# Turning 64-column tiles into both halves of PSUM instead of first doubling them in SBUF, in a two-block transformer kernel

## The chip, the core and the metric

The kernel runs on one core of one Trainium2 chip. Its time is the device time of one execution in microseconds, given as the median of three runs. The engines named below are PE (TensorE, the matrix engine), ACT (ScalarE), DVE (VectorE), POOL (GpSimd) and SP (SyncE, which here issues the weight transfers). SBUF is the on-chip memory with 128 partitions; PSUM holds the results of the matrix engine in eight banks, each 512 f32 numbers wide in every partition.

## The reference, cut to what matters

Sequence length 512, model width 1024, head size 64, everything in f32. The first block has differential attention, an attention with compressed, selected and windowed keys ("NSA") and an MLP. The second block has forget-gated attention ("fox") and sliding-window attention with sinks ("swa"), whose four key heads are each shared by four query heads. Two pieces matter here.

```
# 1. compression of the NSA keys (kc) and values (vc): 4 groups of 64 columns, windows of 32 tokens, stride 16
k_cmp = compress(kc.reshape(B, S, G, HEAD_DIM), cmp_pos_k[l], cmp_k_w1[l], cmp_k_w2[l])
v_cmp = compress(vc.reshape(B, S, G, HEAD_DIM), cmp_pos_v[l], cmp_v_w1[l], cmp_v_w2[l])
#    for each group and each of 31 windows: the 32 x 64 numbers of the window, plus a position term,
#    times a [2048, 256] matrix, GELU, times a [256, 64] matrix

# 2. scores of the swa block: 16 query heads against 4 key heads
logits = jnp.einsum('bnqhgd,bnkhd->bnhgqk', qb, k_band) * scale
```

## The kernel before, in words

Every large product is split into groups of 512 output columns; a group has two units of weights, each 512 rows deep. ACT and DVE split the weights of a unit into a high and a low part (`spl`), and PE multiplies three times (high-high, high-low, low-high). A unit is 48 such matmuls on PE. The results of a group lie in four PSUM banks, and ACT copies ("evicts") them into `QKV`, where tokens lie along the partitions. There are two slots for unit weights and two sets of four banks, so each engine works in an order that is written out by hand, one list per engine. Semaphores tie the lists together. `run(...)` walks the groups of a stage. Its arguments `at` and `between` put other work ahead of a group or behind a unit.

The stage `nsa_in` has the groups pd0, pd1, kc, nq0, nq1, ks, kw and ng, numbered 0 to 7. The group kc brings 256 columns of keys and 256 of values to be compressed. The compression needs, for each of the 32 token positions of a window, the 64 columns of a token along the partitions. Two token positions are packed together: one in partitions 0 to 63, the next in partitions 64 to 127, so that its first layer is 16 matmuls deep instead of 32 for each half of the hidden columns. The kernel before gets the packing in this way:

- ACT evicts kc twice (`token_twice`, line 760), so that every 64-column group lies twice side by side, in 128 columns of `QKV` (1536 to 2560).
- PE turns these 128-column tiles (`tokens_across`, line 2113): 16 transposes for the keys after unit 0 of group nq0, and 16 for the values after unit 0 of group ks. Both halves of the partitions then hold the same 64 columns.
- DVE copies windows out of partitions 0 to 63 (`inputs`, line 1696) and ACT those out of partitions 64 to 127 (`inputs`, line 1057), 16 copies each of 64 x 124 numbers. A constant, the position term, is added. The partitions of ACT's half are read one token further (`window`).
- PE may not begin group nq1 (number 4) before the first set of copies is done, and not group kw (number 6) before the second (`gathered`), since these groups write the banks that the copies read. The first layer (`first_layer`, line 2124) is 32 matmuls, once for the keys and once for the values.

In the swa block the same doubling is done for keys. Each of the eight units of that attention works on two query heads, one in partitions 0 to 63 and one in 64 to 127, against one key head that must lie in both halves. POOL copies the four key heads twice into columns 2560 to 3072 (`keys_twice`, line 1962), between the normalization of the keys and that of the first query group. PE turns a 128-column tile (`turn`, line 2453) for queries (argument `i` = 0) in every unit and for keys (`i` = 1) in every second unit. The first three such turns stand ahead of the loop; the others stand inside it, two steps ahead of the unit that needs them. PE waits for POOL's copies through the semaphore `k_twice`.

Of the kernel before, what the change touches and what calls it, by code (L numbers as in the profile page):

```python
# [22 lines left out]
ALU = mybir.AluOpType  # L23
ACT = mybir.ActivationFunctionType
AX = mybir.AxisListType

P = 128
S = 512
NT = S // P
D = 1024  # L30
KT = D // P
HD = 64
# [223 lines left out]
def program(nc, I, out):  # L256
    RUNS = plan()
    LAST = {a: [g for r in RUNS.values() for g in r if g["by"] == a][-1]["freed"] for a in ("act", "dve")}
    with ExitStack() as ctx:
# [12 lines left out]
        def sem(name):  # L272
            return ctx.enter_context(nc.semaphore(name))
# [118 lines left out]

        ck_zero, k_twice, c_xk2 = sem("ck_zero"), sem("k_twice"), sem("c_xk2")
        x_parked, x_back = sem("x_parked"), sem("x_back")
# [12 lines left out]
        def c_bank(k):  # L407

            return 4 * ((RUNS["nsa_in"][0]["group"] + k) % 2)
# [84 lines left out]
        def row_bank(name):  # L494

            return 4 * (1 - RUNS["merge"][0]["group"] % 2) + 3 if name == "merge" else 4 * (SIDE[name]["group"] % 2) + 3

        def token_twice(t):

            return QKV[:, t, 1536:2560].rearrange("p (g r d) -> p g r d", r=2, d=HD)  # L500

        def window(i, k, r):

            b, rows, o = c_bank(6 if i else 4), slice(HD * r, HD * r + HD), 2 * k + r
            return (XK[rows, k], PS[rows, b:b + 4, o:o + 1 + CMP_STRIDE * (N_CMP - 1):CMP_STRIDE],
                    POS[rows, i, k:k + 1])

# [167 lines left out]
        def _(act):  # L675
# [48 lines left out]
            def evict(g):  # L724
# [29 lines left out]
                if then[0] in ("norm", "plain"):  # L754
                    k = g["late"]
                    act.wait_ge(*row_count(k))
                    for t in range(NT):
                        if g["name"] == "kc":
                            for r in range(2):
                                last = act.activation(token_twice(t)[:, :, r],  # L760
                                                      PS[:, b0 + t].rearrange("p (g d) -> p g d", d=HD),
                                                      ACT.Copy, scale=RST[:, k, t:t + 1])
                            continue
                        last = act.activation(QKV[:, t, then[1]:then[1] + W], PS[:, b0 + t], ACT.Copy,  # L764
                                              scale=RST[:, k, t:t + 1])
                    last.then_inc(freed["act"], 1)
# [282 lines left out]

            def inputs(i):  # L1050

                act.wait_ge(c_tr, i + 1)
                if i:
                    act.wait_ge(c_hid, 1)
                for k in range(16):
                    dst, src, add = window(i, k, 1)
                    act.activation(dst, src, ACT.Identity, bias=add).then_inc(c_xk2, 1)

            def hidden(i):
# [49 lines left out]
            def lambdas():  # L1109
# [7 lines left out]
            run(RUNS["nsa_in"], primed=True, at={3: lambda: narrow_hi(0, 48), 7: compressed},  # L1117
                between={3: lambda: inputs(0), 4: lambda: hidden(0), 5: lambda: inputs(1), 6: keys_out_values_in})
            compressed_branch()
# [20 lines left out]
        def _(dve):  # L1140
# [548 lines left out]
            def inputs(i):  # L1689

                dve.wait_ge(c_tr, i + 1)
                if i:
                    dve.wait_ge(c_hid, 1)
                for k in range(16):
                    dst, src, add = window(i, k, 0)
                    dve.tensor_scalar(dst, src, add, None, ALU.add).then_inc(c_xk, 1)  # L1696

# [99 lines left out]
        def _(pool):  # L1797
# [157 lines left out]

            def keys_twice():

                pool.wait_ge(n_done, RUNS["swa_in"][0]["normed"] + 1)
                keys = QKV[:, :, 1024:1280].rearrange("p t (h d) -> p t h d", d=HD)
                both = QKV[:, :, 2560:3072].rearrange("p t (h r d) -> p t h r d", r=2, d=HD)  # L1960
                for r in range(2):
                    last = pool.tensor_copy(both[:, :, :, r], keys)
                last.then_inc(k_twice, 1)

            def clear_narrow(last):
# [22 lines left out]
            attend_beside(FOX)  # L1988
            run(RUNS["swa_in"][:1])
            keys_twice()  # L1990
            run(RUNS["swa_in"][1:])
            attend_beside(SWA)
# [3 lines left out]
        def _(pe):  # L1996
# [109 lines left out]
            def tokens_across(i):  # L2106


                pe.wait_ge(freed["act"], RUNS["nsa_in"][4 if i else 2]["freed"])
                for g in range(GROUPS):  # L2110
                    b, c = c_bank(6 if i else 4) + g, 1536 + 512 * i + P * g
                    for t in range(NT):
                        last = pe.transpose(PS[:, b, P * t:P * t + P], QKV[:, t, c:c + P], IDF[:])
                last.then_inc(c_tr, 1)

            def first_layer(i):
                b = c_bank(7 if i else 5) + 2 * i
                pe.wait_ge(freed["act"], RUNS["nsa_in"][5 if i else 3]["freed"])
                pe.wait_ge(w1_full, 16 * (4 if i else 3))
                for m in range(2):  # L2120
                    for k in range(16):
                        pe.wait_ge(c_xk, 16 * i + k + 1)
                        pe.wait_ge(c_xk2, 16 * i + k + 1)
                        last = pe.matmul(PS[:, b, 124 * m:124 * m + 124], W1[:, k, P * m:P * m + P],
                                         XK[:, k].rearrange("p g n -> p (g n)"), start=(k == 0), stop=(k == 15),
                                         skip_group_check=True)
                last.then_inc(c_hid, 1)
# [202 lines left out]
            def attend_beside(a):  # L2330
# [117 lines left out]
                def turn(m, i):  # L2448
                    for t in range(NT):
                        bank, col = (first_bank(a, m, i), P * t) if m < 2 else (turn_bank(a, X_BANK), P * t) if a.is_diff \  # L2450
                            else (turn_bank(a, PT_BANK + t // 2), 256 + P * (t % 2))
                        c = 2560 + P * a.keys_of(m) if i and a.is_swa else 1024 * i + P * m
                        last = pe.transpose(PS[:, bank, col:col + P], QKV[:, t, c:c + P], IDF[:])
                    last.then_inc(s["tk" if i else "tq"], 1)
# [22 lines left out]
                pe.wait_ge(n_done, last_in[{"diff": 3, "fox": 4, "swa": 1}[a.name]]["normed"] + 1)  # L2477
                if a.is_swa:
                    pe.wait_ge(k_twice, 1)
                for m, i in a.first_turns()[:3]:  # L2480
# [32 lines left out]

            def gathered(i):
                pe.wait_ge(c_xk, 16 * i + 16)
                pe.wait_ge(c_xk2, 16 * i + 16)

            pe.wait_ge(loads, 16 * N_LOADS)
            run(RUNS["nsa_in"], at={4: lambda: gathered(0), 5: lambda: pe.wait_ge(c_gelu, 1), 6: lambda: gathered(1)},
                between={(0, 0): lambda: back(KT - 1), (3, 0): lambda: tokens_across(0), (4, 0): lambda: first_layer(0),  # L2520
# [63 lines left out]
```

## Time and profile before

| | |
|---|---|
| median of 3 runs | 1770.33 us (1769.92 to 1773.02) |
| the profiled execution's own time | 1769.92 us |
| its span in the profile | 1768.1 us |
| PE busy | 1678.7 us, 95% of the span, 9314 matmul records |
| DVE, ACT, POOL busy | 933.9, 726.6 and 383.9 us |
| mean granted PE clock | 0.966 of full speed |

Times in the profile are microseconds from the start of the span. A row of a timeline gives the start, the time from the start of the first to the end of the last instruction of a merged group, the engine, the line in the code, what is written and read, the shape, how many records (x16), and in brackets how long the engine had been idle and what ended that. On PE consecutive matmuls overlap at their ends, so the pace of a group is best read from its start to the start of the next group. In the names of a matmul's operands the moving one stands first, the stationary one second; "128\*64" is a stationary operand of 128 rows and 64 columns. A plain f32 matmul leaves two records, a transpose or one of the split matmuls leaves one. The granted clock (PEclk) is 1.00 at the full 2.4 GHz and 0.50 at 1.2 GHz.

### The profile page before, as it was taken

How to read it: one execution, taken by the hardware profiler on the slowest of the kernel's cores; microseconds unless marked ns; L12 is line 12 of the kernel's file. 1: busy time of each engine (PE TensorE's matmuls, PEld its weight loads, DVE VectorE, ACT ScalarE, POOL GpSimd, SP SyncE). 2: the span in 40 equal slices, each digit the busy share in tenths (PEclk: the TensorE clock that was granted, in tenths of full speed). 3: DMA queues.
4: the chain of work that ended last, by engine and by line, in shares of the span. 5: the costliest groups of instructions: out<-in, count | busy, mean ns of one | idle time of the engine just before them, and what ended most of it. 6: DMA issues, size and time to landing. Idle time of an engine off the chain costs nothing.

```text
span 1768.1 us, 24731 instructions
## 1 busy us (share of the span) xinstructions
PE 1678.7 (95%) x9314; PEld 1318.8 (75%) x9314; DVE 933.9 (53%) x1675; ACT 726.6 (41%) x1643; POOL 383.9 (22%) x517
## 2 busy tenths in 40 slices
PE   7999998998879998999999999999999989997989
PEld 6887667887755555888888888888887767885757
DVE  3785674356346666344443244234836774457772
ACT  4324553143336665224332133133325553434550
POOL 5451332023125663011000000000113330022330
PEclk9999998999959999999999999999999998998979
DMA  7222002423012222322322333223230004230111
GB/s 187 96 78 90 25 25 83 143 93 122 1 42 58 62 59 67 126 102 83 95 97 99 101 101 104 96 77 138 96 97 25 26 25 143 96 95 2 49 49 48
DMA packets 107205, 141.38 MB, mean 80 GB/s; under 512 B 30348, under 2 KB 55204, under 8 KB 106848
## 3 DMA queue, kind: packets, MB, share of 16 engines
q1 hardware_dynamic: 106032, 139.10, 24.6%
q0 software_dynamic: 992, 0.86, 0.5%
q8 instruction: 69, 1.13, 0.3%
q14 instruction: 32, 0.26, 0.0%
q10 hardware_dynamic: 80, 0.02, 0.0%
HBM read 125.24 MB, written 4.24 MB: 73 GB/s over the span
## 4 chain that ended last, share of the span: by engine, by line
PE 67%; DVE 11%; issue 10%; ACT 9%; POOL 3%; DMA 0%; ACTq 0%; SPq 0%; POOLq 0%; DVEq 0%
PE ps L2010 50%; PE ps L2462 3%; PE ps L2245 2%; PE ps L2266 2%; ACT pbd L948 2%; DVE spl L1163 2%; DVE nm L1491 2%; PE ps L2281 1%; PE ps L2419 1%; ACT pb L892 1%; DVE qkt L1509 1%; PE ps L2443 1%; ACT qkt L969 1%; PE ps L2351 1%; ACT pts L956 1%
## 5 line engine op out<-in xcount | busy, mean ns | idle before, releaser
L2010 PE MATMUL ps<-spl,ht 128*128 128x512 f32 x2496 | 578.4, 393 | 10.3 <-DVE xk L1696 5.9
L2010 PEld LDWEIGHTS ps<-spl,ht 128*128 128x128 f32 x2496 | 472.7, 190 | 110.1 <-DVE xk L1696 6.3
L1186 DVE TENSOR_TENSOR spl<-raw,spl 128x1024 fp32r<-128x1024 f32 x168 | 222.1, 1364 | 396.3 <-ACT spl L721 396.3
L721 ACT ACTIVATE spl<-raw 128x1024 fp32r<-128x1024 f32 x168 | 168.5, 1052 | 463.5 <-PE ps L2010 437.2
L2010 PE MATMUL ps<-ht,spl 128*128 128x512 f32 x960 | 220.4, 391 | 2.0 <-DVE spl L1186 2.0
L2010 PEld LDWEIGHTS ps<-ht,spl 128*128 128x128 f32 x960 | 181.2, 189 | 40.5 <-issue 2.9
L2010 PE MATMUL ps<-spl,uu 128*128 128x512 f32 x768 | 174.7, 389 | 0.0
L2010 PEld LDWEIGHTS ps<-spl,uu 128*128 128x128 f32 x768 | 144.1, 188 | 29.8
L2462 PE MATMUL ps<-ht,spl 128*128 128x512 f32 x576 | 155.2, 408 | 2.7 <-DVE mx L1546 2.6
L1872 POOL TENSOR_TENSOR sq<-qkv 128x2048 f32<-128x2048 f32 (+1 forms) x15 | 51.5, 3434 | 326.0 <-ACT qkv L764 311.4
L2462 PEld LDWEIGHTS ps<-ht,spl 128*128 128x128 f32 x576 | 102.7, 190 | 23.8 <-DVE mx L1546 4.8
L1968 POOL MEMSET nws<- 128x2048 f32 x2 | 3.6, 1812 | 426.6 <-PE ps L2010 385.1
L1903 POOL TENSOR_TENSOR pb<-pb,rg 128x512 f32<-128x512 f32 (+3 forms) x128 | 89.4, 720 | 5.0
L1491 DVE TENSOR_REDUCE nm<-ps 128x1 f32<-128x512 f32 (+2 forms) x192 | 81.2, 450 | 8.9 <-PE ps L2368 6.5
L892 ACT ACTIVATE pb<-ps,nm 128x512 f32<-128x512 f32 (+3 forms) x128 | 66.4, 528 | 29.2 <-DVE nm L1411 29.2
L2351 PE MATMUL ps<-qkt 64*128 64x256 f32 (+3 forms) x576 | 68.0, 343 | 9.8 <-DVE qkt L1509 9.6
L1411 DVE TENSOR_REDUCE nm<-ps 128x1 f32<-128x512 f32 (+3 forms) x128 | 56.9, 486 | 35.7 <-PE ps L2250 35.6
L2351 PEld LDWEIGHTS ps<-qkt 64*128 64x128 f32 x576 | 43.4, 192 | 43.2 <-issue 32.1
L1949 POOL TENSOR_TENSOR pbf<-pbf,rr 128x512 f32<-128x512 f32 (+3 forms) x64 | 48.8, 783 | 121.1 <-DVE rr L1498 121.1
L1881 POOL TENSOR_TENSOR sq<-qkv,st 128x1024 f32<-128x1024 f32 (+3 forms) x22 | 49.1, 2253 | 63.6 <-DVE qkv L1236 63.6
L2443 PE MATMUL ps<-pts,qkv 128*64 128x128 f32 x544 | 47.8, 303 | 14.3 <-ACT pts L956 11.7
L1163 DVE SCALAR_TENSOR_TENSOR spl<-raw,spl 128x256 fp32r<-128x256 f32 x80 | 45.4, 576 | 23.9 <-ACT spl L698 23.1
(311 smaller groups left out, 2223.5 us busy)
## 6 DMA issues: line engine op xcount, KB each, us to landing
raw<-w_in SPq DMA_DIRECT2D x30, 1024.0 KB, 5.1
raw<-w_mlp_up SPq DMA_DIRECT2D x16, 1024.0 KB, 5.3
raw<-w_mlp_down SPq DMA_DIRECT2D x16, 1024.0 KB, 5.0
raw<-w_in_a SPq DMA_DIRECT2D x16, 1024.0 KB, 5.4
raw<-w_in_b SPq DMA_DIRECT2D x8, 1024.0 KB, 5.5
raw<-w_proj_diff SPq DMA_DIRECT2D x4, 1024.0 KB, 6.8
stq<-qkv SPq DMA_DIRECT2D x16, 256.0 KB, 2.7
stq<-qkv SPq DMA_DIRECT2D x32, 128.0 KB, 2.5
```

The costliest lines, as they stand in the source:

```text
L721: act.activation(SPL[:, n % 2, HI, 2 * k:2 * k + 2], RAW[:, n % 2, 2 * k:2 * k + 2], ACT.Copy).then_inc(hi_done, 4)
L892: last = act.activation(p, PS[:, 2 * (idx % 2) + h, 0:w], ACT.Exp, bias=NM[:, m.slot, h, t:t + 1], accum_out=LS[:, m.slot, h, t:t + 1])
L1163: last = dve.scalar_tensor_tensor(wide(SPL[:, n % 2, LO])[:, k], wide(RAW[:, n % 2])[:, k], gain, wide(SPL[:, n % 2, HI])[:, k].bitcast(F3 ...
L1186: dve.tensor_tensor(SPL[:, n % 2, LO, 2 * k:2 * k + 2], RAW[:, n % 2, 2 * k:2 * k + 2], SPL[:, n % 2, HI, 2 * k:2 * k + 2].bitcast(F32), A ...
L1411: dve.tensor_reduce(top, bank[:, 0:w], AX.X, ALU.max, negate=True).then_inc(s["mx"], 1)
L1491: dve.tensor_reduce(NM[:, m % 2, h, t:t + 1], bank[:, 0:w + a.sink], AX.X, ALU.max, negate=True)\
L1872: pool.tensor_tensor(SQ[:, :, 0:w], QKV[:, :, col:col + w], QKV[:, :, col:col + w], ALU.mult)\
L1903: last = pool.tensor_tensor(p, p, RG[:, m.slot, h, t:t + 1].to_broadcast([P, w]), ALU.mult)
L2010: last = pe.matmul(PS[:, b0 + b], left[:, x], right[:, y], start=(kt == 0 and i == 0), stop=(kt == UK * g["units"] - 1 and i == 2))
L2351: pe.matmul(PS[:, score_bank(a, n, h), 0:w], QKT[r, m % 2, 0, x, P * t:P * t + P], QKT[r, a.keys_of(m) % 2, 1, y, P * a.first_key(t):P * t ...
L2443: last = pe.matmul(PS[HD * h:HD * h + HD, turn_bank(a, PV_BANK), P * t:P * t + P], QKV[:, j, v:v + HD], PTS[h][:, n % 2, o:o + P], start=( ...
L2462: last = pe.matmul(PS[:, side_bank(a, k)], wide(SPL[:, n % 2, x])[:, kt, cols], HT[:, y, kt], start=(kt == 0 and j == 0), stop=(kt == KT - ...
```

## The change

The doubling in SBUF goes away. Where both halves of the partitions must hold the same 64 columns, PE now does two operations on the 64-column tile. A transpose writes partitions 0 to 63, and an ordinary f32 matmul against the identity writes partitions 64 to 127.

```
 def tokens_across(i):
-    pe.wait_ge(freed["act"], RUNS["nsa_in"][4 if i else 2]["freed"])
+    kc = RUNS["nsa_in"][2]
+    pe.wait_ge(freed["act"], kc["freed"])
+    if i:
+        pe.wait_ge(freed["act"], RUNS["nsa_in"][4]["freed"])
     for g in range(GROUPS):
-        b, c = c_bank(6 if i else 4) + g, 1536 + 512 * i + P * g
+        b = c_bank(6 if i else 4) + g
+        src = QKV[:, :, 1024 + 256 * i + HD * g:1024 + 256 * i + HD * g + HD]
         for t in range(NT):
-            last = pe.transpose(PS[:, b, P * t:P * t + P], QKV[:, t, c:c + P], IDF[:])
+            n = P - (t == NT - 1)
+            pe.transpose(PS[0:HD, b, P * t + 1:P * t + 1 + n], src[0:n, t], IDF[0:n, 0:n])
+            last = pe.matmul(PS[HD:P, b, P * t:P * t + P], src[:, t], IDF[:], start=True, stop=True,
+                             skip_group_check=True)
```

The transposed half is written one column further, so both token positions of a window stand in the same columns, and one copy over all 128 partitions takes both. DVE does all the copies, and ACT's `inputs` is gone:

```
 dve.wait_ge(c_tr, i + 1)
 if i:
     dve.wait_ge(c_hid, 1)
+b = c_bank(6 if i else 4)
 for k in range(16):
-    dst, src, add = window(i, k, 0)
-    dve.tensor_scalar(dst, src, add, None, ALU.add).then_inc(c_xk, 1)
+    src = PS[:, b:b + 4, 2 * k + 1:2 * k + 2 + CMP_STRIDE * (N_CMP - 1):CMP_STRIDE]
+    dve.tensor_scalar(XK[:, k], src, POS[:, i, k:k + 1], None, ALU.add).then_inc(c_xk, 1)
```

ACT's double eviction of kc becomes the ordinary one. `keys_twice` on POOL is gone with its semaphore, and the turn of the swa keys is changed like the other:

```
-                        if g["name"] == "kc":
-                            for r in range(2):
-                                last = act.activation(token_twice(t)[:, :, r],
-                                                      PS[:, b0 + t].rearrange("p (g d) -> p g d", d=HD),
-                                                      ACT.Copy, scale=RST[:, k, t:t + 1])
-                            continue
...
-            run(RUNS["swa_in"][:1])
-            keys_twice()
-            run(RUNS["swa_in"][1:])
+            run(RUNS["swa_in"])
...
-                        c = 2560 + P * a.keys_of(m) if i and a.is_swa else 1024 * i + P * m
-                        last = pe.transpose(PS[:, bank, col:col + P], QKV[:, t, c:c + P], IDF[:])
+                        if i == 0 or not a.is_swa:
+                            c = 1024 * i + P * m
+                            last = pe.transpose(PS[:, bank, col:col + P], QKV[:, t, c:c + P], IDF[:])
+                            continue
+                        k = QKV[:, t, 1024 + HD * a.keys_of(m):1024 + HD * a.keys_of(m) + HD]
+                        pe.transpose(PS[0:HD, bank, col:col + P], k, IDF[:])
+                        last = pe.matmul(PS[HD:P, bank, col:col + P], k, IDF[:], start=True, stop=True,
+                                         skip_group_check=True)
```

How this stands on PE at two places. First, in `nsa_in`, from the end of unit 0 of nq0 to the first layer for the keys (`xk` is the gathered windows, `w_88` the first layer's weights, `spl` and `ht` the operands of the large products). Before:

```order
L2010 MATMUL ps<-spl,ht 128x512 x144
L2113 MATMUL ps<-idf,qkv 128x128 x16
L2010 MATMUL ps<-spl,ht 128x512 x96
L2124 MATMUL ps<-xk,w_88 128x124 x32
L2010 MATMUL ps<-spl,ht 128x512 x96
```

And now, where the two lines 2083 and 2084 alternate 16 times, of which the first and the last stand here:

```order
L1975 MATMUL ps<-spl,ht 128x512 x144
L2083 MATMUL ps<-idf,qkv 64x128
L2084 MATMUL ps<-idf,qkv 64x128
...
L2083 MATMUL ps<-idf,qkv 64x127
L2084 MATMUL ps<-idf,qkv 64x128
L1975 MATMUL ps<-spl,ht 128x512 x96
L2095 MATMUL ps<-xk,w_88 128x124 x32
L1975 MATMUL ps<-spl,ht 128x512 x96
```

Each set of 16 transposes has become 16 transposes of half the width and 16 matmuls, and the place in the row is the same. Second, in the loop of the swa block, at one of the three key turns that stand inside it (`pts` is the transposed probabilities, `pbs` the probabilities, `ht` and `spl` the gate's product that runs beside). Before:

```order
L2443 MATMUL ps<-pts_69,qkv 64x128
L2453 MATMUL ps<-idf,qkv 128x128 x4
L2419 MATMUL ps<-idf,pbs_83 128x128 x2
L2462 MATMUL ps<-ht,spl 128x512 x6
L2351 MATMUL ps<-qkt 128x256 x6
```

And now:

```order
L2414 MATMUL ps<-pts_69,qkv 64x128
L2428 MATMUL ps<-idf,qkv 64x128
L2429 MATMUL ps<-idf,qkv 64x128
...
L2428 MATMUL ps<-idf,qkv 64x128
L2429 MATMUL ps<-idf,qkv 64x128
L2390 MATMUL ps<-idf,pbs_83 128x128 x2
L2439 MATMUL ps<-ht,spl 128x512 x6
L2322 MATMUL ps<-qkt 128x256 x6
```

Four transposes have become four pairs of a transpose and a matmul. Nothing else on PE changes its place.

## Rows read from the trace of the kernel before

**Rows 1.** The page: the span, and busy time of each engine.

```profile
span 1768.1 us, 24731 instructions
PE 1678.7 (95%) x9314; PEld 1318.8 (75%) x9314; DVE 933.9 (53%) x1675; ACT 726.6 (41%) x1643; POOL 383.9 (22%) x517
```

**Rows 2.** Timeline of PE, 355 to 440 us: the compression inside `nsa_in`.

```profile
362.46 1.91 PE L2113 MATMUL ps<-idf,qkv 128*128 128x128 f32 x16
364.13 22.05 PE L2010 MATMUL ps<-spl,ht 128*128 128x512 f32 x96
386.02 7.30 PE L2124 MATMUL ps<-xk,w 128*128 128x124 f32 x64
393.08 22.02 PE L2010 MATMUL ps<-spl,ht 128*128 128x512 f32 x96
...
416.60 11.14 PE L2010 MATMUL ps<-spl,ht 128*128 128x512 f32 x48
433.65 6.62 PE L2010 MATMUL ps<-spl,ht 128*128 128x512 f32 x22 [5.90 <-DVE xk L1696]
```

**Rows 3.** Chain that ended last, 400 to 440 us: start, duration, what.

```profile
418.12 6.70 POOL sq L1881 x2
...
429.45 4.15 DVE xk L1696 x16
```

**Rows 4.** Timeline of ACT, 340 to 445 us.

```profile
354.27 4.71 ACT L760 ACTIVATE qkv<-ps,rst 128x512 f32<-128x512 f32 x8
363.02 2.01 ACT L721 ACTIVATE spl<-raw 128x1024 fp32r<-128x1024 f32 x2 [4.04 <-PE ps L2010]
```

**Rows 5.** Groups of DVE by shape: xcount | busy us, mean ns | idle.

```profile
L1621 DVE TENSOR_TENSOR ys<-y,ys 128x512 fp32r<-128x512 f32 x8 | 4.9, 681 | 0.0
...
L1669 DVE TENSOR_TENSOR crem<-cum,c 16x512 f32<-16x512 f32 x1 | 0.7, 678 | 0.0
```

**Rows 6.** Timeline of PE, 1388 to 1398 us, in the fox block.

```profile
1390.87 1.09 PE L2443 MATMUL ps<-pts,qkv 128*64 128x128 f32 x16
1391.89 0.88 PE L2419 MATMUL ps<-idf,pbf 128*128 128x128 f32 x6
```

**Rows 7.** Timeline of PE, 1268 to 1272 us: turning 16 columns.

```profile
1269.72 0.60 PE L2536 MATMUL ps<-idf,fl 128*16 128x128 f32 x4
1270.08 2.30 PE L2010 MATMUL ps<-spl,ht 128*128 128x512 f32 x9
```

**Rows 8.** Stretches: PE, PEld, DVE, ACT, POOL busy, PEclk, DMA share, GB/s.

```profile
434.00:436.00 2.00, 2.00 (x6) 1.52 (x6) 2.00 (x2) 0.00 (x0) 0.28 (x1) 0.50 0.00 0
436.00:438.00 2.00, 2.00 (x9) 1.64 (x8) 2.00 (x6) 0.00 (x0) 0.00 (x0) 0.88 0.29 23
```

**Rows 9.** The same view, 697 to 701 us.

```profile
697.00:699.00 2.00, 0.06 (x2) 0.00 (x0) 1.90 (x3) 2.00 (x3) 0.00 (x0) 1.00 0.02 2
699.00:701.00 2.00, 1.93 (x5) 1.59 (x6) 2.00 (x2) 2.00 (x5) 0.00 (x0) 0.58 0.36 39
```

**Rows 10.** Timeline of POOL, 1530 to 1620 us.

```profile
1553.76 2.03 POOL L1962 COPY qkv<-qkv 128x1024 f32<-128x1024 f32 x2 [5.40 <-DVE qkv L1260]
1563.82 3.60 POOL L1872 TENSOR_TENSOR sq<-qkv 128x2048 f32<-128x2048 f32 x1 [8.02 <-ACT qkv L764]
```

**Rows 11.** Timeline of PE, 1530 to 1620 us: the start of the swa attention.

```profile
1581.29 1.47 PE L2453 MATMUL ps<-idf,qkv 128*128 128x128 f32 x12
...
1602.58 1.01 PE L2351 MATMUL ps<-qkt 64*128 64x256 f32 x6 [8.90 <-DVE qkt L1509]
```

**Rows 12.** Timeline of PE, 1640 to 1656 us: a key turn in the loop.

```profile
1648.48 0.65 PE L2453 MATMUL ps<-idf,qkv 128*128 128x128 f32 x4
1648.97 0.38 PE L2419 MATMUL ps<-idf,pbs 128*128 128x128 f32 x2
...
1652.51 0.63 PE L2419 MATMUL ps<-idf,pbs 128*128 128x128 f32 x4 [0.31 <-POOL pbs L1949]
```

**Rows 13.** Waits of PE, 1600 to 1770 us: total, times, longest.

```profile
PE ps L2419 <- POOL pbs L1949: 0.6, 2, 0.3
```

More of the change, by code:

```diff
@@ L391, in need @@
             return BESIDE[k], n + (0 if a.is_diff else IN_DIFF[k]) + (IN_FOX[k] if a.is_swa else 0)
-        ck_zero, k_twice, c_xk2 = sem("ck_zero"), sem("k_twice"), sem("c_xk2")
+        ck_zero = sem("ck_zero")
         x_parked, x_back = sem("x_parked"), sem("x_back")
@@ L496, in row_bank @@
             return 4 * (1 - RUNS["merge"][0]["group"] % 2) + 3 if name == "merge" else 4 * (SIDE[name]["group"] % 2) + 3
[L498 to L506, printed above, removed]
         def reach(eng, s, value):
@@ L1048, in split_y @@
                     act.activation(YS[:, HI, k], Y[:, k], ACT.Copy).then_inc(y_hi, 1)
[L1050 to L1057, printed above, removed]
             def hidden(i):
@@ L1117, in _ @@
             run(RUNS["nsa_in"], primed=True, at={3: lambda: narrow_hi(0, 48), 7: compressed},
-                between={3: lambda: inputs(0), 4: lambda: hidden(0), 5: lambda: inputs(1), 6: keys_out_values_in})
+                between={4: lambda: hidden(0), 6: keys_out_values_in})
             compressed_branch()
@@ L1954, in attend_beside @@
                     root(KT - 1)
[L1956 to L1963, printed above, removed]
             def clear_narrow(last):
@@ L2122, in first_layer @@
                         pe.wait_ge(c_xk, 16 * i + k + 1)
-                        pe.wait_ge(c_xk2, 16 * i + k + 1)
                         last = pe.matmul(PS[:, b, 124 * m:124 * m + 124], W1[:, k, P * m:P * m + P],
@@ L2477, in attend_beside @@
                 pe.wait_ge(n_done, last_in[{"diff": 3, "fox": 4, "swa": 1}[a.name]]["normed"] + 1)
-                if a.is_swa:
-                    pe.wait_ge(k_twice, 1)
                 for m, i in a.first_turns()[:3]:
@@ L2512, in keys_out_values_in @@
                 narrow(RUNS["nsa_in"][-1], 0)
-            def gathered(i):
-                pe.wait_ge(c_xk, 16 * i + 16)
-                pe.wait_ge(c_xk2, 16 * i + 16)
             pe.wait_ge(loads, 16 * N_LOADS)
-            run(RUNS["nsa_in"], at={4: lambda: gathered(0), 5: lambda: pe.wait_ge(c_gelu, 1), 6: lambda: gathered(1)},
+            run(RUNS["nsa_in"], at={4: lambda: pe.wait_ge(c_xk, 16), 5: lambda: pe.wait_ge(c_gelu, 1),
+                                    6: lambda: pe.wait_ge(c_xk, 32)},
                 between={(0, 0): lambda: back(KT - 1), (3, 0): lambda: tokens_across(0), (4, 0): lambda: first_layer(0),
```

## The prediction

> **What bounds the kernel now.** The page comes first: PE is busy 1678.7 of 1768.1 us [rows 1], so an operation put on PE costs its own time unless PE waits soon after it, and one taken off another engine is worth only what PE waited for it. The timeline of PE through the compression comes next. PE runs without a gap from the first transposes at 362.46 to the end of ks at 427.7, then stands idle 5.90 us until DVE's window copies are done [rows 2]. The chain of waits shows what made these copies late. It passes through POOL's products for the rotation of nq1 (418.12) to the copies at 429.45 [rows 3]: DVE first finishes the normalization of nq1, which PE completed before it turned the values, and then turns to the copies. So the end of the wait hangs on PE's end of nq1, not on the turn of the values that follows it. ACT's half of the copies is never named. The third place is the swa block: PE waits 8.90 us before its first scores and almost nothing inside the loop [rows 11 to 13].
>
> **What a turn costs, before and now.** The 16 transposes take 364.13 - 362.46 = 1.67 us, 0.104 each [rows 2]. Now each tile has a transpose and an f32 matmul of 128 columns, which leaves two records. The nearest price of such a record is the first layer's: 64 records in 393.08 - 386.02 = 7.06 us, 0.110 each, so a matmul takes 0.22 [rows 2]. No row shows a transpose of 64 columns. One of only 16 columns is no cheaper than a whole one: four in 1270.08 - 1269.72 = 0.36 us, 0.09 each [rows 7]. I take 0.104, half the width being no saving.
>
> The open question is whether the two overlap. They write different halves of the partitions. Matmuls that do so already stand in the trace: 16 records of L2443, which alternate between the halves, take 1391.89 - 1390.87 = 1.02 us, 0.064 each [rows 6]. That is little over half of the 0.110 of a record that fills all 128 columns. Two at a time they would take 16 x 0.055 = 0.88, and 0.14 us is what such a group pays once. So two matmuls in different halves run at the same time. If a transpose in one half overlaps with the matmul in the other in the same way, a pair lasts as long as the half with more to do: 0.22. If not, 0.104 + 0.22 = 0.324. With nearly nothing to tell them apart I choose the row of the same shape, which overlaps: 0.22 a pair, and 0.1, most of that 0.14, once for a group.
>
> Here the Trainium skill speaks against the change. Its page "TensorEngine Tiling (Array Packing)", section "Key Properties", says that changing the tiling mode drains the engine, and section "Gotcha 2: Feature Incompatibilities" that column tiling excludes transpose mode for f32 input. By the second, the transposes would have to leave the tiled mode, and by the first each pair would pay for draining twice. The 16-column f32 transposes, with their usual cost, speak against it [rows 7], but none of them stands next to a tiled matmul. So I keep it as a rival below.
>
> **The change part by part.**
> - *Turn of the keys to be compressed.* 16 x 0.22 + 0.1 = 3.6 us instead of 1.67: +1.95 us. PE has no gap before it reaches the end of nq1, which starts the chain to the 433.65 wait. So the whole 1.95 is exposed. It moves everything behind it. Bounds: 48 records at 0.064 are 3.1, +1.4; without overlap 16 x 0.324 + 0.1 = 5.3, +3.6.
> - *Turn of the values.* The same +1.95, but after the end of nq1 and before the 5.90 us idle, whose end does not depend on it: 0. Some 4.0 us of idle are left (2.3 without overlap). Were that cover gone, it would cost as much as the first.
> - *The clock.* PE's granted clock is 0.50 from 434 to 436 and on average 0.88 from 436 to 438, so the work from 433.65 to about 436.5 ran at 1.2 GHz, where the same work takes twice its time: some 1.4 us lost [rows 8]. A shorter idle time could save it. But elsewhere the clock fell after a stall of only about 2 us: idle from 697 to 699 at 1.00, then 0.58 [rows 9]. I take 0; bounds -1.4 and +0.3.
> - *Window copies.* DVE keeps its 16 per set, now over 128 partitions instead of 64. DVE's time does not follow the partitions: 512 columns take 678 ns on 16 partitions and 681 ns on 128 [rows 5]. So 4.15 us stays, 0. At the other end, if twice the partitions took twice as long, the second set would add 4.15 us, all exposed. ACT's 32 copies go, and nobody waited for them: 0. The first layer now waits for one semaphore per step instead of two. Its 0.110 per record is 0.006 above a transpose's 0.104, so at most 128 x 0.006 = 0.8 us is to be had. I take 0.
> - *Eviction of kc.* ACT does 4 instead of 8, saving half of 4.71 us; ACT then sat idle 4.04 us until PE freed a weight slot [rows 4]. Nobody waited: 0.
> - *POOL's doubling of the swa keys.* 2.03 us at 1553.76, after which POOL idled 8.02 us until an eviction [rows 10]. 0, and PE's removed wait had long been satisfied.
> - *First key turn of swa.* One third of the 12 transposes at 1581.29: +0.5, hidden behind the 8.90 us that end with DVE [rows 11]. 0; it costs 0.5 (0.9 without overlap) if uncovered.
> - *Three key turns in the loop.* Each takes 1648.97 - 1648.48 = 0.49 now [rows 12], and 4 x 0.22 + 0.1 = 0.98 then: +0.49, three times 1.47. PE has next to no gap in the loop, so this is exposed, except that one step after two of the three PE waits 0.3 us for POOL's scaled probabilities (1652.51 is one), 0.6 in all, which start from scores PE has done before the turn [rows 12, 13]. 1.47 - 0.6 = +0.9. Bounds: 3 x (12 x 0.064 - 0.49) - 0.6 = +0.2 and, without overlap, 3 x (1.296 + 0.1 - 0.49) - 0.6 = +2.1.
>
> **Sum.** 1.95 + 0.9 = +2.85 us on a profiled execution of 1769.92 (span 1768.1 and 1.8 around it). That execution was 0.4 below the median of 1770.33. I forecast the median: 1773.2 us.
>
> **Rivals.**
> - *No overlap* (slower). A transpose and a matmul in different halves run one after the other. Place: the key turn and the three turns in the loop. Price: 3.6 + 2.1 = +5.7 us, 1776.0. For it: no row shows the two kinds side by side. Against: the same shape overlaps among matmuls [rows 6]. With p us a pair the sum is 16p - 1.57 + 12p - 1.77 = 28p - 3.34, so it decides from p = 0.25 on, where the sum passes 3.5 us.
> - *Draining* (slower). Each pair pays what a group of matmuls in halves pays once, 0.14 us [rows 6], on top of no overlap: 0.464 a pair, +5.85 for the key turn, 3 x (1.856 + 0.1 - 0.49) - 0.6 = +3.8 in the loop: +9.65, 1780.0. The value turn stays just covered: 5.85 against 5.9. This is what the page of the Trainium skill named above would lead to.
> - *Cheap records and a saved clock* (not slower). Every record at 0.064: +1.4 + 0.2 = +1.6. If then the shorter idle keeps the clock, -1.4: 1770.5. Against: two records in a row into the same half have no row at that pace, and the stall of 2 us speaks against the clock [rows 9].
> - *Copies that grow with the partitions* (slower): 2.85 + 4.15 = +7.0, 1777.3. Rows 5 leave it little.
>
> **Chances and range.** Overlap 0.50, no overlap 0.27, draining 0.11, cheap 0.09, growing copies 0.03. A measurement tells 0.2% from no change, 3.5 us. The forecast at +2.85 lies inside it by only 0.7, and phases of the clock and the spread of the runs move it by about 1, so 0.13 of its 0.50 go to slower. With no overlap 0.25, draining 0.11 and growing copies 0.02, slower gets 0.51. Faster by 3.5 us needs more than any edit here frees on PE: 0.04. The same: 0.45. The range runs from 1771.0 to 1778.0; it holds the forecast, the case without overlap and most of the growing copies, and leaves out draining and the best of cheap. The forecast's own range is 1771.8 to 1774.5.
>
> **What would show it.** In the trace after, the key turn lasts 3.6 us from its start to the next large matmul (5.3: no overlap; 7 and more: draining). The idle time before kw shrinks from 5.9 to about 4.0 and still ends with DVE's copies, whose 16 last 4.15 us. The clock dips there as before. The swa stage has a wait of about 8.4 us before its first scores, key turns of 1.0 us in the loop, and the two 0.3 us waits for POOL are gone. I am wrong if PE's new wait is for ACT or POOL at a place that had none, or if the turn of the values shows up in the start of kw.

## The result, and the profile after

The changed kernel takes 1781.78 us (median of 5, 1779.92 to 1784.85). The kernel before, run beside it, takes 1772.39 (median of 5). By the medians that is +9.4 us. The ratio over all executions, 30 of the changed kernel, is 1.0058, interval 1.0047 to 1.0069: 8.3 to 12.2 us slower. The forecast was 1773.2, the range 1771.0 to 1778.0, so the time lies outside. About 2 us of the distance come from the kernel before, which the forecast took at 1770.33. The profiled execution took 1782.82, its span is on the first line of the page:

```profile
span 1781.0 us, 24819 instructions
PE 1702.4 (96%) x9410; PEld 1329.2 (75%) x9410; DVE 933.5 (52%) x1675; ACT 717.1 (40%) x1607; POOL 382.4 (21%) x515
```

Against [rows 1], PE has 96 more records and 23.7 us more busy time. That is 0.25 per record; the forecast's turns added 1.95 us for 32 records, 0.06 each, and without overlap 0.11. ACT and POOL have less to do, as the change says. The timeline of PE through the compression, which answers to [rows 2], shows where the time is:

```profile
365.27 0.27 PE L2083 MATMUL ps<-idf,qkv 128*64 128x128 f32 x1
365.47 0.43 PE L2084 MATMUL ps<-idf,qkv 128*64 128x128 f32 x2
365.84 0.30 PE L2083 MATMUL ps<-idf,qkv 128*64 128x128 f32 x1
366.07 0.43 PE L2084 MATMUL ps<-idf,qkv 128*64 128x128 f32 x2
...
374.36 0.43 PE L2084 MATMUL ps<-idf,qkv 128*64 128x128 f32 x2
374.72 22.07 PE L1975 MATMUL ps<-spl,ht 128*128 128x512 f32 x96
...
425.55 0.27 PE L2083 MATMUL ps<-idf,qkv 128*64 128x128 f32 x1
...
435.00 22.07 PE L1975 MATMUL ps<-spl,ht 128*128 128x512 f32 x96
456.91 0.54 PE L2103 MATMUL ps<-w2s,hid 128*124 128x64 f32 x4
```

L2083 is the transpose, L2084 the matmul beside it (two records). Read the starts, since the durations hold the pipeline's depth. From a transpose to its matmul it is 0.20 to 0.23 us, from the matmul to the next transpose 0.36 or 0.37: 0.59 a pair. The 16 pairs of the keys last 374.72 - 365.27 = 9.45 us, where 1.67 stood and 3.6 was forecast. The 16 of the values last the same. The 5.90 us idle before kw is gone: the 96 large matmuls of ks and kw follow each other without a gap.

The weight loads of PE (PEld, LDWEIGHTS) show where the time between the two kinds lies:

```profile
365.05 0.11 PEld L2083 LDWEIGHTS ps<-idf,qkv 128*64 128x64 f32 x1
365.47 0.19 PEld L2084 LDWEIGHTS ps<-idf,qkv 128*64 128x64 f32 x2 [0.32 <-issue]
365.83 0.11 PEld L2083 LDWEIGHTS ps<-idf,qkv 128*64 128x64 f32 x1 [0.17 <-issue]
```

The loads sit idle 0.32 and 0.17 us ahead of the last two of these rows, waiting for nothing that the profile names. The load of each kind starts only at the time (365.47, 365.83) at which PE's own record begins, with nothing loaded ahead while the other kind streams. The very first transpose is different: its weights are loaded at 365.05, 0.22 us before it starts at 365.27, while the large matmuls ahead of it still run. The chain of waits, which went through POOL and DVE before [rows 3], now stays on PE:

```profile
425.71 0.11 PE ps L2083
425.82 0.36 PE ps L2084 x2
```

DVE's 16 copies for the values, now over 128 partitions, and ACT's eviction and next work, which answer to [rows 3 to 5]:

```profile
439.93 4.15 DVE L1672 TENSOR_SCALAR xk<-ps,pos 128x124 f32<-128x124 f32 x16
```

```profile
357.09 2.40 ACT L748 ACTIVATE qkv<-ps,rst 128x512 f32<-128x512 f32 x4
365.55 2.00 ACT L711 ACTIVATE spl<-raw 128x1024 fp32r<-128x1024 f32 x2 [6.06 <-PE ps L1975]
```

The copies take 4.15 us as before and end at 444.08, some 2 us before PE comes to kw near 446.0. ACT does its eviction in half the time and waits 6.06 instead of 4.04. And since PE did not stall, its clock (the 1.00 behind POOL's busy time) stays full at the place of [rows 8]:

```profile
446.00:448.00 2.00, 2.00 (x10) 1.66 (x9) 0.60 (x1) 1.69 (x2) 0.00 (x0) 1.00 0.03 8
```

In the swa attention, in answer to [rows 11, 12]:

```profile
1612.37 1.01 PE L2322 MATMUL ps<-qkt 64*128 64x256 f32 x6 [6.95 <-DVE qkt L1484]
...
1659.61 0.28 PE L2428 MATMUL ps<-idf,qkv 128*64 128x128 f32 x1
...
1661.95 0.44 PE L2390 MATMUL ps<-idf,pbs 128*128 128x128 f32 x2
...
1732.10 10.12 PE L1975 MATMUL ps<-spl,ht 128*128 128x512 f32 x35
```

A key turn takes 2.34 us instead of 0.49, and the wait before the first scores is 6.95 instead of 8.90: the first turn's extra 1.95 is hidden there, as forecast. The waits of PE no longer name POOL ([rows 13]).

Two more starts on PE in the kernel before, the second layer and the end of swa's loop, serve to lay the traces side by side:

```profile
446.00 0.54 PE L2132 MATMUL ps<-w2s,hid 128*124 128x64 f32 x4
...
1719.18 11.04 PE L2010 MATMUL ps<-spl,ht 128*128 128x512 f32 x39
```

The traces drift apart like this, each by the start of the same instruction: at the keys' first transpose by 2.8 us (stretches of half clock in the first 170 us that lie differently in these two executions, ahead of any change), after them by 10.6, at the second layer (446.00 and 456.91) by 10.9, at the first scores of swa by 9.8, at the end of its loop (1719.18 and 1732.10) by 12.9. So the keys' turn costs +7.8, the values' turn +0.3 net, the swa loop +3.1. That is 11.2 us, inside the interval. Between the second layer and swa's first scores the changed kernel gains 1.1 us in these two executions. It does so in work that the change doesn't touch, for the most part where the granted clock changes (near 508 and 1470 us); it is not counted.

### The profile page after: what moved, and what is told of

Same layout as the page of the kernel before. It is cut to its first block, busy times and chain, and to the rows that moved or that the text cites. A ratio compares the mean times of both kernels' runs of the same rounds, so it can differ in the third digit from the quotient of the medians.

```text
span 1781.0 us, 24819 instructions
## 1 busy us (share of the span) xinstructions
PE 1702.4 (96%) x9410; PEld 1329.2 (75%) x9410; DVE 933.5 (52%) x1675; ACT 717.1 (40%) x1607; POOL 382.4 (21%) x515
## 4 chain that ended last, share of the span: by engine, by line
PE 77%; DVE 9%; ACT 8%; issue 4%; POOL 1%; DMA 0%; ACTq 0%; SPq 0%; POOLq 0%; DVEq 0%
PE ps L1975 55%; PE ps L2439 3%; PE ps L1967 2%; PE ps L2216 2%; PE ps L2237 2%; ACT pbd L932 2%; DVE nm L1466 1%; PE ps L2252 1%; DVE spl L1138 1%; PE ps L2322 1%; PE ps L2390 1%; PE ps L2414 1%; ACT pb L876 1%; ACT pbf L932 1%; PE ps L2095 1%
## 5 line engine op out<-in xcount | busy, mean ns | idle before, releaser
L2414 PE MATMUL ps<-pts,qkv 128*64 128x128 f32 x544 | 48.0, 304 | 13.6 <-ACT pts L940 10.6
```

The costliest lines, as they stand in the source:

```text
L2414: last = pe.matmul(PS[HD * h:HD * h + HD, turn_bank(a, PV_BANK), P * t:P * t + P], QKV[:, j, v:v + HD], PTS[h][:, n % 2, o:o + P], start=( ...
```

## The experiments

The traces say what a pair costs, not why. Theory A (as the expectations call it) is that each step between a transpose and an ordinary matmul costs by itself. Its rivals: the transpose with 64 columns is slow, going back and forth between the halves of the partitions is slow, or any change of kind is slow, at full width too. All times are medians, but for two kernels that ran once; the kernel before took 1772.2 to 1772.4 on the same chips.

**Grouping the kinds.** Per four tiles first all transposes, then all matmuls, in the compression and in swa.

```
                     for t in range(NT):
                         pe.transpose(PS[0:HD, ...], src[0:n, t], IDF[0:n, 0:n])
+                    for t in range(NT):
                         last = pe.matmul(PS[HD:P, ...], src[:, t], IDF[:], ...)
```

> The changed kernel with the same operations in another order: for each four tiles first the four transposes into partitions 0 to 63, then the four matmuls into 64 to 127, in both turns of the compression and in all swa key turns. In the trace of the changed kernel a pair took 0.59 us, 0.23 from transpose to matmul and 0.36 from matmul to transpose, against 0.104 + 0.22 without anything between. Theory A, the going from a transpose to a matmul and back costs some 0.13 us each time: two such steps per four tiles instead of eight, so four tiles take 4 x 0.104 + 8 x 0.11 + 2 x 0.13 = 1.56 us instead of 2.37, the key turn 6.2 instead of 9.45 us, and the kernel is about 5 us faster than the changed one (about 1777). Theory B, each 64-column operation is slow in itself: four tiles stay at 2.4 us, the time at 1782. Theory C, going from one half of the partitions to the other costs: the same as A.

1774.58 us, ratio to before 1.0016 (1.0006 to 1.0026). The same operations in another order save 7 of the 9 us; 5 were expected. Its timeline of PE:

```profile
362.31 0.60 PE L2083 MATMUL ps<-idf,qkv 128*64 128x128 f32 x4
362.84 1.09 PE L2085 MATMUL ps<-idf,qkv 128*64 128x128 f32 x8
363.86 0.63 PE L2083 MATMUL ps<-idf,qkv 128*64 128x128 f32 x4
...
368.59 9.79 PE L1975 MATMUL ps<-spl,ht 128*128 128x512 f32 x42
...
438.03 9.36 PE L1975 MATMUL ps<-spl,ht 128*128 128x512 f32 x40 [1.19 <-DVE xk L1672]
```

Four tiles take 363.86 - 362.31 = 1.55 to 1.58 us with two steps, where eight steps took 4 x 0.59 = 2.36. So a step costs (2.36 - 1.58) / 6 = 0.13 us. What is left is 1.58 - 0.26 = 1.32 for four tiles, 0.33 each: a 64-column transpose of 0.11 and a matmul of 0.22, one after the other. The transpose itself isn't slow. The last row is the start of kw: 1.19 us of idle are left of 5.90, since the values' turn now fills more of it.

**Two matmuls.** Both halves by ordinary matmuls, at all sites; no transposes.

```
-                        pe.transpose(PS[0:HD, ...], src[0:n, t], IDF[0:n, 0:n])
+                        pe.matmul(PS[0:HD, ...], src[0:n, t], IDF[0:n, 0:n], start=True, stop=True, ...)
```

> The changed kernel with both halves written by ordinary f32 matmuls against the identity, in the same order tile by tile. There is no transpose left among the 64-column operations, but the halves still alternate. Theory A (a step between transpose and matmul costs): no step is left, both halves overlap as in L2414's groups at 0.064 us a record, so 16 tiles take 64 x 0.064 = 4.1 us instead of 9.45, four tiles 1.0 to 1.1 instead of 2.4, and the kernel comes to about 1773, 9 us faster than the changed one and within 1 or 2 us of the kernel before. Theory B (the 64-column operations are slow in themselves, 0.36 us a matmul): 32 x 0.36 = 11.6 us, slower than the changed kernel by 2 us or more. Theory C (going to the other half costs 0.13): 32 x (0.22 + 0.13) = 11 us, slower too.

1773.21 us, ratio 1.0008 (0.9998 to 1.0017): +1.0 us over the 1772.22 of the kernel before. That it lies on the forecast's 1773.2 is chance, since the forecast added 2.85 to 1770.33. The price of a pair is what this kernel puts to the test, and its timeline of PE shows it:

```profile
364.38 0.32 PE L2083 MATMUL ps<-idf,qkv 128*64 128x128 f32 x1
364.39 0.32 PE L2085 MATMUL ps<-idf,qkv 128*64 128x128 f32 x1
...
368.02 2.35 PE L1975 MATMUL ps<-spl,ht 128*128 128x512 f32 x9
```

The two halves start 0.01 us apart and a pair takes 0.22: 3.64 us for all 16, where 3.6 was forecast for the change. Going back and forth between halves costs nothing. So overlap is real for two matmuls, and missing for a transpose and a matmul. Theory B and Theory C are both out.

**Steps at full width.** The kernel before, with every second of the compression's whole-width transposes as a plain matmul.

```
-                        last = pe.transpose(PS[:, b, ...], QKV[:, t, c:c + P], IDF[:])
+                        if t % 2: last = pe.matmul(PS[:, b, ...], QKV[:, t, c:c + P], IDF[:], ...)
+                        else: last = pe.transpose(PS[:, b, ...], QKV[:, t, c:c + P], IDF[:])
```

> The kernel before, in whose two turns of the compression every second one of the 16 full-width (128-column) transposes is an ordinary f32 matmul against the identity, into all 128 partitions; output unchanged. Read from the start of the 16 operations to the next large matmul. If the step between a transpose and a matmul costs 0.13 us whatever the width: 8 x 0.104 + 8 x 0.22 + 16 x 0.13 = 4.7 us. If it costs only where the operations fill half of the columns: 2.6 us. The time: +3.0 or +1 us over the kernel before.

1770.40 us (one execution, within the spread of the kernel before, so that the time says nothing here). Timeline of PE, and then of its weight loads:

```profile
362.83 0.27 PE L2117 MATMUL ps<-idf,qkv 128*128 128x128 f32 x1
362.94 0.39 PE L2114 MATMUL ps<-idf,qkv 128*128 128x128 f32 x2
363.17 0.27 PE L2117 MATMUL ps<-idf,qkv 128*128 128x128 f32 x1
...
365.27 0.39 PE L2114 MATMUL ps<-idf,qkv 128*128 128x128 f32 x2
365.41 0.94 PE L2010 MATMUL ps<-spl,ht 128*128 128x512 f32 x3
```

```profile
363.06 0.14 PEld L2117 LDWEIGHTS ps<-idf,qkv 128*128 128x128 f32 x1
```

A pair takes 0.33 or 0.34 us, 0.11 + 0.22, with 16 steps among them, and all of them take 365.41 - 362.83 = 2.58 us, as the second case had it (2.6 against 4.7). At full width a step is free. The next kind's weights are loaded before the other's stream ends (363.06, for a record that starts at 363.17). That is what the changed kernel's loads don't do.

**Steps inside one half.** In the lower half transpose and matmul in turn (T M T M), then four matmuls for the upper half; compression only.

```
+                        if t % 2: pe.matmul(PS[0:HD, ...], src[0:n, t], IDF[0:n, 0:n], ...)
+                        else: pe.transpose(PS[0:HD, ...], src[0:n, t], IDF[0:n, 0:n])
+                    for t in range(NT):
                         last = pe.matmul(PS[HD:P, ...], src[:, t], IDF[:], ...)
```

> The changed kernel, in whose two turns of the compression the lower half of each four tiles is written by transpose, matmul, transpose, matmul, and then the upper half by four matmuls. All steps between transpose and matmul but one per four tiles are now inside one half of the partitions. Theory A (the step between the kinds costs 0.13 us among 64-column operations, whichever half they write): four steps per four tiles, 2 x 0.104 + 2 x 0.22 + 3 x 0.22 + 4 x 0.13 = 1.8 to 2.0 us for four tiles. Theory E (it costs only where the step also changes the half): one such step, 1.4 to 1.6 us. The time is not the question: about 2 us below the changed kernel.

1779.36 us (one execution). Timeline of PE:

```profile
365.23 0.27 PE L2087 MATMUL ps<-idf,qkv 128*64 128x128 f32 x1
365.43 0.43 PE L2084 MATMUL ps<-idf,qkv 128*64 128x128 f32 x2
365.79 0.30 PE L2087 MATMUL ps<-idf,qkv 128*64 128x128 f32 x1
366.02 0.32 PE L2084 MATMUL ps<-idf,qkv 127*64 127x127 f32 x1
366.03 0.32 PE L2089 MATMUL ps<-idf,qkv 128*64 128x128 f32 x1
...
367.04 0.30 PE L2087 MATMUL ps<-idf,qkv 128*64 128x128 f32 x1
```

L2087 and L2084 write the same half, and yet the steps are the 0.20 to 0.23 and 0.36 of the changed kernel. At 366.02 a lower and an upper matmul start together. Four tiles take 367.04 - 365.23 = 1.81 us, in the 1.8 to 2.0 of Theory A and not the 1.4 to 1.6 of Theory E. What costs is the change of kind among 64-column operations, whichever half it writes.

The ends of the turns in the changed kernel narrow this down. Ahead of the first transpose stand large matmuls, which are ordinary ones at full width. That change of kind is free: the weights are loaded ahead (365.05), and the transpose starts 0.23 us after the last large matmul, which is the pace of the large ones (22 us for 96). Behind the last 64-column matmul stands a large matmul again, which is no change of kind. Yet it comes only 0.36 us later (374.36 to 374.72), as late as a transpose would, where the same step at full width takes 365.41 - 365.27 = 0.14. The 0.14 us that a group of L2443 pays once [rows 6] is of the same kind, and there the neighbours behind are transposes of 128 columns. So the price hangs on going into and out of 64-column ordinary matmuls. A 64-column transpose stands on the side of the full-width operations: from them to it nothing is paid.

**The three places alone.** On the kernel before, the transpose and matmul pair only in swa's key turns (without the doubling), only in the values' turn, only in the keys' turn. The edit is the change's own line for one place, here the keys':

```
+                        if i == 0:
+                            pe.transpose(PS[0:HD, b, ...], QKV[:, t, c:c + HD], IDF[:])
+                            last = pe.matmul(PS[HD:P, b, ...], QKV[:, t, c:c + HD], IDF[:], ...)
```

> The kernel before with the change made in the swa block alone (key turns of transpose and matmul, POOL's doubling gone), the compression as before. By the trace of the changed kernel the three key turns in the loop take 2.37 instead of 0.49 us each, 5.6 in all, less 0.6 and 0.2 of waits that disappear and less what the first, covered turn does not add: I expect +3 to +5 us over the kernel before (1775 to 1777), and so +5 to +6 of the whole +9.4 for the compression. Rival: POOL's 2 us are worth something after all, and the swa block is neutral.

> The kernel before, with only the turn of the values changed into 16 pairs of a transpose and a matmul; doubling, copies and everything else as before. The turn then takes 9.45 instead of 1.67 us, +7.8, against 5.90 us of idle time before the group kw. By the trace of the changed kernel 1.9 us stick out, and the clock loss of 1.4 us or more goes with the wait: +0 to +1 us over the kernel before. Rival: it is exposed in full, +7.8.

> The kernel before, with only the turn of the keys to be compressed changed into 16 pairs of a transpose and a matmul. Theory: all of it is exposed, 9.45 - 1.67 = +7.8 us over the kernel before (1780), the wait of 5.9 us before the group kw stays as it is, and only moves. Together with the swa turns (+3) and the value turn (0 to +1) this is 11 to 12 us against the measured 9.4, so something of 2 us is given back; if that is at the key turn, this kernel shows +6.

swa alone: 1775.17, ratio 1.0016 (1.0006 to 1.0026), +2.9 us. The values' turn alone: 1772.24, ratio 0.9995 (0.9985 to 1.0004), nothing. The keys' turn alone: 1780.46, ratio 1.0050 (1.0035 to 1.0066), +8.1 by the medians. With the keys' turn alone PE still waits for DVE, with the values' turn alone it doesn't. Timelines of PE, first of the keys' turn alone, then of the values':

```profile
442.02 8.24 PE L2010 MATMUL ps<-spl,ht 128*128 128x512 f32 x29 [5.91 <-DVE xk L1696]
```

```profile
427.29 22.06 PE L2010 MATMUL ps<-spl,ht 128*128 128x512 f32 x96
```

The expectation asked whether some 2 us are given back at the keys' turn; they aren't. So 7.8 us of work put in ahead of the end of nq1 move the idle time, and do not shrink it. The same 7.8 us behind it fill the 5.9 us, and the clock that is not lost pays for most of the rest. The three add up to 11 us, within the interval of the whole.

**What the idle time is worth.** The 5.90 us end with DVE's copies for the values, so ACT now does them: all 32 of the values, in the order of the tokens, and then in another order, the 16 of the lower half first. Both start from the kernel before.

```
-                for k in range(16):
-                    dst, src, add = window(i, k, 1)
+                for k in range(16):                # second version: these two
+                    for r in range(1 - i, 2):      # loops exchanged
+                        dst, src, add = window(i, k, r)
```

> The kernel before (doubling in SBUF kept), with the 32 window copies of the values all on ACT and none on DVE; DVE's second set is gone, and PE's second wait is for ACT alone. In the trace of before, ACT reached its copies at 417.25 us and DVE at 429.45, and PE stood idle 5.90 us for DVE's, after which it ran at half clock for 2.8 us or longer. ACT's 32 copies at 0.258 us each are 8.3 us, done at 425.5, before PE ends the group ks at 427.7. Theory D, the late copies alone make this wait: it goes, with the clock loss of 1.4 to 3 us, so 6 to 8 us faster than before, about 1765. Rival: another wait takes its place (the split of kw's weights, or the eviction of ks behind the longer ACT work), and less than 3 us are left.

> As e6 (the kernel before with all window copies of the values on ACT), but ACT does the 16 copies of partitions 0 to 63 first and then the 16 of 64 to 127, instead of going back and forth. In e6 its 32 copies took 12.08 us, 0.378 each, against 0.258 in the kernel before, where all 16 of a set are in one half; PE still waited 1.49 us for them. Theory F, ACT overlaps a copy with the next only while both lie in the same half of the partitions: 32 x 0.258 = 8.3 us, done at 425.7 before PE ends ks, no wait left, 1 to 1.5 us faster than e6, about 1765. Theory G, 0.378 us is what the copies cost whenever another engine works as well, and their order does not matter: as e6, 1766.4.

In the order of the tokens: 1766.39, ratio 0.9969 (0.9957 to 0.9981). By halves: 1763.52, ratio 0.9951 (0.9937 to 0.9964). The second beats both kernels, by 8.8 us the one before. ACT and PE in each, first in the order of the tokens:

```profile
417.43 12.08 ACT L1058 ACTIVATE xk<-ps,pos 64x124 f32<-64x124 f32 x32
```

```profile
429.56 11.18 PE L2012 MATMUL ps<-spl,ht 128*128 128x512 f32 x48 [1.49 <-ACT xk L1058]
```

Then by halves:

```profile
418.35 8.25 ACT L1058 ACTIVATE xk<-ps,pos 64x124 f32<-64x124 f32 x32
```

```profile
417.82 22.02 PE L2013 MATMUL ps<-spl,ht 128*128 128x512 f32 x96
439.68 0.54 PE L2136 MATMUL ps<-w2s,hid 128*124 128x64 f32 x4
```

The same 32 copies take 0.378 us each when they alternate between the halves and 0.258 when they don't. A single copy lasts some 0.36 us in both, so that copies in one half overlap and alternating ones don't, as Theory F has it. The first order leaves a wait of 1.49 us, the second none. By the medians the second is 2.9 us faster where 1 to 1.5 were expected; the two ran on different chips. From the start of ks to the second layer it is 446.00 - 416.60 = 29.4 us before, and 439.68 - 417.82 = 21.9 here: 7.5 us, which are the 5.9 of idle time and the 1.4 of clock and little more. The rest of the 8.8 has no place in the traces; single executions of one kernel differ by as much.

## Why the prediction was wrong

- **What a turn costs** is the step that failed: "With nearly nothing to tell them apart I choose the row of the same shape, which overlaps: 0.22 a pair". The row of L2443 [rows 6] is a true price, but of two operations of one kind; two matmuls cost just that in the experiment, 0.22. A transpose beside a matmul costs 0.59: 0.11 and 0.22 one after the other, and 0.13 at each of the two steps. (The prediction's 0.104 is a little low: it divides 1.67 us by 16, but the large matmul's record starts before the last transpose's turn is over. The traces have 0.109 from one transpose to the next.) The no-overlap rival (0.324) lacked the steps. The draining rival had the mechanism and about the right size of one drain, 0.14, but counted it once a pair, not at both steps. It gave +9.65 in total, inside the measured 8.3 to 12.2, but partly by luck: its pair was too cheap by 0.13, and it missed what the loop hides. That draining empties the engine is a reading of the rows; what they show is that the next weights aren't loaded while the other kind streams. That the two kinds never overlap follows from the paces above.

  The Trainium skill, page "TensorEngine Tiling (Array Packing)", says in "Key Properties" that a change of the tiling mode drains the engine, and in "Gotcha 2: Feature Incompatibilities" that column tiling and transpose mode exclude each other for f32 input. By these two a 64-column transpose must leave the tiled mode and each step must pay, while nothing is paid at full width. The trace agrees: 0.13 us a step among 64-column operations in either half, 0 at full width, and 0 from a full-width matmul into a 64-column transpose. I held [rows 7] against this rule, where transposes of 16 columns cost no more than usual, but those rows have no tiled matmul beside them, so they could not speak on the step. The chance of 0.11 was the error of judgement.
- **Turn of the keys**: all of it exposed, as said; +7.8 us for +1.95. That is 5.85 of the 8.35 us by which the +11.2 of the traces miss the forecast's +2.85. The rest is the loop (+3.1 for +0.9) and the values' turn (+0.3), which had the same pair too cheap.
- **Turn of the values**: 0 was forecast, +0.3 came, but not as worked out. With 9.45 us the cover of 5.9 is gone and 1.9 stick out; the clock, which no longer falls, gives 1.4 back. The sign of wrongness that I named, the turn showing up in the start of kw, did happen.
- **The clock**: 0 was taken because it had fallen elsewhere after a stall of 2 us, and it was wrong for the changed kernel: no idle time is left before kw, the clock stays full, and the bound of -1.4 came true. In the case that the forecast had in mind it would have been right: with two matmuls 3.75 us remain, and it fell as before. With the kinds grouped 1.19 us remain, and it did not.
- **Copies, eviction, POOL's doubling, first swa turn**: all 0 as forecast; 4.15 us for the 16 copies of 128 partitions, waits of 6.06 and 6.95 in place of 4.04 and 8.90.
- **Key turns in the loop**: 3 x (2.34 - 0.49) = 5.6 us were put in and only 3.1 came out. I counted 0.6 of cover from the view of waits [rows 13]. There is more, in pieces that this view doesn't list. In the kernel before, the timeline after the key turn of [rows 12] goes on:

```profile
1649.38 1.66 PE L2462 MATMUL ps<-ht,spl 128*128 128x512 f32 x6
...
1654.84 0.29 PE L2368 MATMUL ps<-causal,id 64*128 64x128 bf16 x4
1655.23 0.66 PE L2443 MATMUL ps<-pts,qkv 128*64 128x128 f32 x8
```

L2462 starts 0.41 after the 1648.97 of [rows 12], and the second pair above lies 0.39 apart. After the change the same pairs of starts stand at 1661.95 and 1662.15, and at 1667.24 and 1667.46: 0.20 and 0.22. With the 0.31 for POOL that is 0.7 us of slack behind this one turn. The waits for DVE's maxima shrank too, from 1.0 us in all to 0.6. So the step that failed here is "PE has next to no gap in the loop": the gaps are there, each too short for the view of waits.

## What to carry to other kernels

On PE a price from a row holds for that order of kinds. Where 64-column f32 matmuls and transposes must stand together, count how often PE goes into and out of the 64-column matmuls, and group them by kind or use one kind: that alone decided between +9.4 us and +2.4 (grouped) or +1.0 (matmuls only). And when an engine idles at the end of a chain, ask who ends the wait and whether an idle engine can do that work: here giving it to ACT was worth 8.8 us, where taking work off ACT and POOL, for which PE had waited next to nothing, shows no gain in the trace.

## What the runs showed of the hardware

- Among f32 operations of 64 columns a step between transpose and matmul costs 0.13 us on PE, in either half; at 128 columns it costs nothing (pair of 0.33). Going from a full-width matmul into a 64-column transpose costs nothing either, while going from a 64-column matmul to a full-width one takes 0.36 us instead of 0.14. Two 64-column matmuls into different halves overlap wholly: 0.22 a pair, as much as one alone. No run here has a transpose into the upper half, so whether two transposes in different halves would overlap isn't shown; nor are steps next to ordinary matmuls of other widths than 64 and 128.
- ACT's copies of 64x124 take 0.378 us when source and destination go back and forth between the halves, and 0.258 in a row within one; a single one lasts some 0.36 either way. DVE takes 4.15 us for 16 of 128 partitions as it did for 16 of 64.
- PE's granted clock after a stall: 1.00 after 1.19 us of idle (kinds grouped) and after 1.49 (copies on ACT). After 3.75 us (two matmuls) it fell to 1.2 GHz. The columns are length, PE busy, granted clock, DMA share and GB/s, first of the grouped kernel, then of two matmuls:

```profile
438.00:441.00 3.00, 2.97 (x13) 1.00 0.03 5
```

```profile
437.00:440.00 3.00, 2.44 (x6) 0.50 0.00 0
440.00:443.00 3.00, 3.00 (x9) 0.54 0.69 212
```

In the latter PE restarts at 437.56 and runs some 5 us at half speed, against some 3 us in the kernel before [rows 8], though the stall was shorter. It doesn't follow the stall's length: with swa alone changed, the same stall of 5.90 us (restart at 436.75) was followed by some 4 us of half clock, and with the full-width steps one of 4.98 us by some 5. Why is left open, with one profile of each; a long low stretch eats part of what a shorter stall saves.
